# Modulation products on four column tiles of the array, their shifts and scales kept as columns, in a two-layer diffusion step

## The reference

```
mod = silu(cond) @ w_mod[l] + b_mod[l]            # 2 layers x (1024 x 6144), 50 MB of weights
sh1, sc1, g1, sh2, sc2, g2 = split(mod, 6)
hn = rmsnorm(x, norm1_g[l]) * (1 + sc1) + sh1
x = x + g1 * mixer(hn)                            # layer 0: RG-LRU and short conv; layer 1: attention
hn = rmsnorm(x, norm2_g[l]) * (1 + sc2) + sh2
x = x + g2 * channel_mixer(hn)                    # layer 0: SwiGLU; layer 1: top-2 of 8 experts
```

## Time and profile before

| | us |
|---|---|
| timed runs | 1918.38, 1922.94, 1922.93 (median 1922.93) |
| profiled execution | 1918.46, span 1916.8 |
| TensorE, VectorE, ScalarE, GpSimd busy | 1765.3, 1119.7, 914.7, 104.1 |
| mean granted TensorE clock | 0.959 of full speed |

### The profile page before, as it was taken

One profiled execution on the slowest core, in us unless ns is written; L12 is line 12 of the kernel. 1 busy time (PEld: TensorE's weight loads), 2 busy tenths in 40 slices (PEclk: granted clock), 3 DMA queues, 4 the chain that ended last, 5 costly groups with the idle time before them and its releaser, 6 DMA issues.

```text
span 1916.8 us, 22046 instructions
## 1 busy us (share of the span) xinstructions
PE 1765.3 (92%) x8208; PEld 1344.4 (70%) x8208; DVE 1119.7 (58%) x1022; ACT 914.7 (48%) x943; POOL 104.1 (5%) x86
## 2 busy tenths in 40 slices
PE   6999989699999969999978999999999999999992
PEld 2444444378888869877366878787878787878781
DVE  0310650443332354245167797979797979797976
ACT  1203210333332242222026686868686868686864
POOL 2211010000000011000000000000000000000001
PEclk9999999899999979998958999999999999999996
DMA  9766547923332372240057899999999999999994
GB/s 298 242 220 220 177 140 257 332 74 132 109 104 62 143 147 95 70 151 1 21 198 258 305 394 351 395 351 395 351 395 350 395 351 395 351 393 352 395 350 149
DMA packets 278410, 472.94 MB, mean 247 GB/s; under 512 B 32876, under 2 KB 133896, under 8 KB 278360
## 3 DMA queue, kind: packets, MB, share of 16 engines
q1 hardware_dynamic: 254704, 438.33, 64.5%
q10 hardware_dynamic: 19160, 20.51, 3.2%
q0 software_dynamic: 4496, 13.41, 1.9%
HBM read 454.28 MB, written 17.93 MB: 246 GB/s over the span
## 4 chain that ended last, share of the span: by engine, by line
PE 80%; DVE 9%; ACT 4%; issue 3%; ACTq 2%; DMA 1%; DVEq 0%; POOL 0%; POOLq 0%
PE ps L1803 26%; PE ps L1816 10%; PE ps L1602 10%; PE ps L1526 8%; PE ps L1567 5%; PE ps L1619 5%; PE ps L1499 4%; PE ps L1658 3%; DVE e_lo L1361 2%; PE ps L1581 2%; ACTq L869 2%; ACT e_hi L994 2%; PE ps L1673 2%; PE ps L1725 1%; PE ps L1697 1%
## 5 line engine op out<-in xcount | busy, mean ns | idle before, releaser
L1361 DVE TENSOR_TENSOR e_lo<-e_raw,e_hi 128x2048 fp32r<-128x2048 f32 (+1 forms) x330 | 690.7, 2115 | 117.6 <-ACT e_hi L994 114.3
L994 ACT ACTIVATE e_hi<-e_raw 128x2048 fp32r<-128x2048 f32 (+1 forms) x330 | 580.6, 1774 | 127.3 <-PE ps L1803 90.4
L1803 PE MATMUL ps<-e_hi,e_x 128*128 128x512 f32 (+1 forms) x1728 | 511.7, 376 | 7.1 <-DVE e_x L1456 7.1
L1803 PEld LDWEIGHTS ps<-e_hi,e_x 128*128 128x128 f32 x1728 | 316.8, 189 | 66.7 <-issue 10.8
L1803 PE MATMUL ps<-e_lo,e_x 128*128 128x512 f32 (+1 forms) x864 | 322.1, 373 | 0.0
L1816 PE MATMUL ps<-e_hi,e_h 128*128 128x512 f32 x792 | 221.8, 391 | 0.0
L1803 PEld LDWEIGHTS ps<-e_lo,e_x 128*128 128x128 f32 x864 | 163.6, 189 | 27.0
L1602 PE MATMUL ps<-split,hi_x 128*128 128x512 f32 (+1 forms) x576 | 171.8, 383 | 5.4 <-DVE lo_x L1247 5.4
L1816 PEld LDWEIGHTS ps<-e_hi,e_h 128*128 128x128 f32 x792 | 147.6, 188 | 29.6
L1526 PE MATMUL ps<-ring,cond 128*2 128x256 f32 x576 | 128.6, 384 | 8.7 <-DMA ring<-in_w_mod_dram 8.7
L1816 PE MATMUL ps<-e_lo,e_h 128*128 128x512 f32 x396 | 122.2, 390 | 0.0
(11 more groups left out here) (236 smaller groups left out, 1896.0 us busy)
## 6 DMA issues: line engine op xcount, KB each, us to landing
e_raw<-in_moe_w_gate_dram SPq DMA_DIRECT2D x94, 1024.0 KB, 11.0
e_raw<-in_moe_w_up_dram SPq DMA_DIRECT2D x92, 1024.0 KB, 11.2
e_raw<-in_moe_w_down_dram SPq DMA_DIRECT2D x90, 1024.0 KB, 11.2
ring<-in_w_mod_dram SPq DMA_DIRECT2D x36, 1024.0 KB, 6.1
mod_extra<-in_w_mod_dram SPq DMA_DIRECT2D x12, 1024.0 KB, 6.4
ring<-in_w_qkv_dram SPq DMA_DIRECT2D x6, 2048.0 KB, 8.9
ring<-in_w_in_dram SPq DMA_DIRECT2D x5, 2048.0 KB, 10.1
ring<-in_ffn_w_gate_dram SPq DMA_DIRECT2D x10, 1024.0 KB, 7.6
```

Of the source, the lines that this page charges most:

```text
L994: act.activation(high_part(c), raw(c), ACT.Copy).then_inc(hi_ok, 1)
L1361: dve.tensor_tensor(low_part(c), raw(c), high_part(c).bitcast(F32), ALU.subtract).then_inc(lo_ok, 1)
L1803: ins = pe.matmul(out, e_x[:, xt, ci, :], wt[:, kk, :], start=(ci == 0 and m == 0), stop=(ci == KC - 1 and m == 2))
```

## The change

The modulation product is laid out anew.

- A unit is 1 MB of 512 columns and half the contraction (four chunks of 128), so the moving rows in DRAM are 2 KB long rather than 1 KB. `cond` is padded with zeros to 32 columns per chunk.
- A block `b` of 512 columns is two units. Chunk k of a unit writes PSUM partitions 32k to 32k+31, which puts it on column tile k of the array. A unit has four products of 512 columns, and each tile adds its two chunks.
- The four partial rows lie in partitions 0, 32, 64, 96 (and the next ones, for the second group). ScalarE copies the whole 128 x 512 bank to `mod_part`. TensorE then sums the partials with a 0/1 matrix (`mod_sums`): for gates as a 2 x 512 row; for shifts and scales with `mod_part` as weights, so that columns come out at once. ScalarE takes these sums to `mod_row` or `modv`.
- GpSimd adds biases to four gate rows and stores those alone; biases of shifts and scales are added as columns.
- Two groups' worth (four blocks) precede the x projection, and four blocks now follow each of x, c, v, b and g. The raw tokens are transposed into `hn_t` early and scaled in place when the columns are there.
- PSUM bank 5 belongs to the sums, and PB becomes 5.

```diff
-GROUP = 4 * 256
+MOD_BLOCKS = 2 * MODS // 512
+LAST_TAKE = 11
-        MOD_SPLIT = {"x": (4, 6), "c": (6, 8), "v": (8, 10), "b": (10, 12), "g": ()}
+        MOD_SPLIT = {"x": (4, 8), "c": (8, 12), "v": (12, 16), "b": (16, 20), "g": (20, 24)}
+        def is_row(b):
+            return b // 2 % 3 == 2
-        PB = 6
+        PB = 5
...
+            def mod_block(b):                                  # SP
+                for n in (2 * b, 2 * b + 1):
+                    if n >= 4:
+                        sp.wait_ge(mod_used, n - 3)
+                    wl, at_ = w_mod[b // 12].rearrange(kview, p=P), b % 12 * 512
+                    sp.dma_start(mod_unit(n), wl[:, n % 2 * 4:n % 2 * 4 + 4, at_:at_ + 512]).then_inc(mod_full[n % 4], 16)
...
+            for r in range(4):                                 # GpSimd
+                at_ = (3 * r + 2) * GROUP
+                pool.dma_start(mod_bias, bias_rows[at_:at_ + GROUP].partition_broadcast(2)).then_inc(mod_bias_in, 16)
+                pool.wait_ge(mod_bias_in, 16 * (r + 1))
+                pool.wait_ge(mod_taken, 3 * r + 2)
                 pool.tensor_tensor(mod_row, mod_row, mod_bias, ALU.add).then_inc(mod_row_ok, 1)
...
+            def take_sums(b):                                  # ScalarE
+                if not is_row(b) and (b % 6 != 3 or b < 6):
+                    return
+                act.wait_ge(mod_sum, b + 1)
+                if is_row(b):
+                    if b >= 6:
+                        act.wait_ge(mod_stored, 16 * (b // 6))
+                    ins = act.activation(mod_row[:, b % 2 * 512:b % 2 * 512 + 512], ps[0:2, 5, :], ACT.Copy)
+                else:
+                    c_ = 8 * (b // 2 - 1)
+                    ins = act.activation(modv[:, c_:c_ + 16, :].rearrange("p m g -> p (m g)"), ps[:, 5, 0:32], ACT.Copy)
+                ins.then_inc(mod_taken, 1)
+            def mod_out(*blocks):
+                for b in blocks:
+                    if b >= 2:
+                        if b != 12:
+                            take_sums(b - 2)
+                        act.wait_ge(mod_sum, b - 1)
+                    act.wait_ge(mod_used, 2 * b + 2)
+                    act.activation(mod_part[:, b % 2, :], ps[:, 6 + b % 2, :], ACT.Copy).then_inc(mod_copied, 1)
...
-                    act.wait_ge(mod_stored, 16 * (2 * MODS // GROUP))
+                    act.wait_ge(mod_stored, 16 * 4)            # gate_in(0)
-            mods_before = {"c": (4, 5), "gate": (6, 7), "g": (10, 11)}
+            mods_before = {"c": (4, 5, 6, 7), "gate": (8, 9, 10, 11), "g": (16, 17, 18, 19)}
-                        mod_out(8 + d)
+                        mod_out(12 + 2 * d, 13 + 2 * d)
+            mod_out(20, 21, 22, 23)
+            take_sums(22)
+            take_sums(23)
             gate_in(0)
...
+            def mod_block(b):                                  # TensorE
+                if b >= 2:
+                    pe.wait_ge(mod_copied, b - 1)
+                for n in (2 * b, 2 * b + 1):
+                    pe.wait_ge(mod_full[n % 4], n // 4 * 16 + 16)
+                    for k in range(4):
+                        ins = pe.matmul(ps[32 * k:32 * k + 32, 6 + b % 2, :], cond[:, n % 2 * 4 + k, :],
+                                        mod_unit(n)[:, k, :], start=(n % 2 == 0), stop=(n % 2 == 1))
+                    ins.then_inc(mod_used, 1)
+            def mod_sums(b):
+                pe.wait_ge(mod_copied, b + 1)
...
+                if is_row(b):
+                    ins = pe.matmul(ps[0:2, 5, :], sum_up, mod_part[:, b % 2, :], start=True, stop=True)
+                else:
+                    for n in range(4):
+                        o = 2 * (4 * (b % 6) + n)
+                        ins = pe.matmul(ps[:, 5, o:o + 2], mod_part[:, b % 2, n * P:(n + 1) * P], sum_up,
+                                        start=True, stop=True)
+                ins.then_inc(mod_sum, 1)
+            def mod_blocks(lo, hi):
+                for b in range(lo, hi):
+                    mod_block(b)
+                    if b > lo:
+                        mod_sums(b - 1)
```

More of the change, by code:

```diff
@@ L85 @@
 C_EXP2, C_ROW2 = C_ROW + 8, C_ROW + 24
-N_CONST = C_ROW2 + 16
+C_SUM = C_ROW2 + 16
+N_CONST = C_SUM + 2
 WORK = 18560
@@ L128, in shape_constants @@
         k[:, C_ROW2:][:, at_] = np.arange(8) * (P * TILES) + P * t
+    for g in range(2):
+        k[g::32, C_SUM + g] = 1.0
     return k
@@ L308, in hybrid_step @@
         mod_ok = sem("mod_ok")
-        mod_copied, mod_bias_in, mod_row_ok, mod_stored, mod_in = (sem("mod_" + n) for n in
-            ("copied", "bias_in", "row_ok", "stored", "rows_in"))
+        mod_copied, mod_sum, mod_taken, mod_bias_in, mod_row_ok, mod_stored = (sem("mod_" + n) for n in
+            ("copied", "sum", "taken", "bias_in", "row_ok", "stored"))
+        raw_dve, raw_act, cond_zero = sem("raw_turn_dve"), sem("raw_turn_act"), sem("cond_zeroed")
         gains_ok = sem("gains_ok")
@@ L521, in fill @@
                 sp.dma_start(dst, src).then_inc(ring_full[slot_of(n)], 16)
[L523 to L535, removed]
+            def mod_block(b):
[4 more added lines that the diff above has]
+                    sp.dma_start(mod_unit(n), wl[:, n % 2 * 4:n % 2 * 4 + 4, at_:at_ + 512]).then_inc(mod_full[n % 4], 16)
+            sp.wait_ge(s_vec, 16 * 13)
+            for b in range(4):
+                mod_block(b)
             win = w_in[0].rearrange(kview, p=P)
@@ L539, in _ @@
                 fill(F_IN + f, slab(F_IN + f), win[:, :, g * 512:(g + 1) * 512])
[L540 to L545, removed]
+                for b in range(*MOD_SPLIT["xcvbg"[f]]):
+                    mod_block(b)
             for f in range(2):
@@ L735, in _ @@
                 rows.append((vec_rows[COL[name]:COL[name] + src.shape[0], 0, :], src))
+            rows.append((vec_rows[0:2 * MODS // P, 1, :], b_mod.rearrange("l (r p) -> (l r) p", p=P)))
             for dst, src in rows:
@@ L895, in _ @@
             act.wait_ge(st_t, 1)
+            act.wait_ge(mod_ok, 2)
             split_high_ffn(0)
@@ L1530, in turn_mod_rows @@
-            def turn_mod_rows(n_rows, count, bank):
-                pe.wait_ge(mod_in, count)
-                for g in range(2):
-                    ins = turn(ps[:, bank, g * P:g * P + n_rows], vec_rows[0:n_rows, g, :])
-                ins.then_inc(vec_t, 1)
+            def mod_block(b):
[7 more added lines that the diff above has]
+                    ins.then_inc(mod_used, 1)
```

160 lines of the change are left out of this document (88 added, 72 removed).

## The result

The changed kernel takes **1884.15 us** (median of four runs, 1881.78 to 1887.33) against 1920.66 for the kernel before in the same comparison (1917.34 to 1922.94): a ratio of 0.9816, 95% interval 0.980 to 0.983. The profiled execution took 1887.33 us. The forecast was 1885. The first residual starts at 328.27, 33.3 us earlier than before; from there to the end the profiled span is 1557.3 us against 1555.2, so the whole gain lies ahead of that residual, as argued. But some of the forecast's sizes are off, in opposite directions, and it took the experiments to show that.

What follows compares the result with a forecast made beforehand. TensorE's modulation products were taken to bound the serial start, with DMA bounding the stages after the change. Stage terms summed to -37.0, plus 4 for clock: -33 on 1918.46 us, 1885 us, range 1870 to 1898 (1866 to 1913 with the clock rival).

Steps and rivals of the forecast that it cites:

- start to x projection: Before the first projection: eight units instead of sixteen and no trip through DRAM, x projection at 42.4 instead of 80.74, -38.3 us.
- after x: Stage after the x projection: refilled units and the next slab bound by their loads, 20.45 us against 27.72, -7.3.
- after c to the last gate: Stage after the c projection: gates wait for ScalarE's copy, table load and evacuations, 28.7 us against 38.9, -10.2.
- last gate to the end of b: From v through b: ScalarE's second direction starts earlier, -7.1; a third b item follows v's first evacuation, +5.2; together -1.9 us.
- after b: Stage after the b projection: the same as after x, bound by loads of units and slab, -7.3 us.
- after g to the gate loads: After g: four blocks, sums, GpSimd's add and the row store now precede ScalarE's gate loads, 28.0 us against 0, +28.0.
- zeroing: ScalarE's nine zeroing DMAs behind the gate loads, ahead of the first FFN split: length left at 37.19 us, no change.
- projections x, c, g: Clock lost after new waits ahead of a projection or product (after x, b, g): 2.7 us at half of three, +4.
- unit's size: TensorE's time for one unit of four products: pairs of records overlap only partly, 1.7 us instead of 3.46.
- side estimate of 1.45 us: TensorE's time for one unit if 3.46 us is divided by the Trainium skill's 2.38 for three column tiles.
- rival with four at once: All four products of a unit overlap, 0.86 us a unit: about -6.7, 1879 us; inside the forecast's 0.62 chance.
- clock rival: TensorE's clock falls in the waits, so refilled units run at half clock: +18, 4 already counted, 1899 us; chance 0.16.

Runs made afterwards that it cites:

- spare products: The changed kernel with unread identity products, two ahead of each refilled unit and four ahead of the slab after x and b: 1878.67 us, ratio 0.979.

## Why the prediction was right, step by step

Measured from the profiles of before and after, in us against the kernel before:

| step | predicted | measured |
|---|---|---|
| start to x projection (80.74 to 43.48) | -38.3 | -37.3 |
| after x (27.7 to 20.8) | -7.3 | -6.9 |
| after c to the last gate (38.9 to 30.4) | -10.2 | -8.6 |
| last gate to the end of b (78.5 to 72.5) | -1.9 | -6.0 |
| after b (27.7 to 21.2) | -7.3 | -6.5 |
| after g to the gate loads (0 to 28.0) | +28.0 | +28.0 |
| zeroing (37.2 to 33.2) | 0 | -4.0 |
| projections x, c, g (predicted: the clock behind three waits) | +4 | +8.1 |
| **first residual** | **-33** | **-33.3** |

The rows measured leave 0.1 over, which lie between the gate loads and the residual.

**The mechanism held.** TensorE's products left the path, DMA took it, the row path after g ran over the store, GpSimd and the zeroing, and the product (279.82, 20.3 after g, predicted 20.45) stayed ahead of the split. (It was to wait for its slab; that landed at 279.5, and the profile puts the last 0.5 us down to ScalarE's take of a gate row.) The prediction named 42 for the x projection, 322 for the split and 329 for the residual: 43.48, 322.55 and 328.27.

**The unit's size was wrong.** The step "those two must follow each other, and products are issued in order, so the second record of one can run beside the first of the next and no more" gave 1.7 us, which is what two tiles measure (1.75). Four tiles measure 0.87. TensorE's weight loads at the start of the stage, in the kernel after:

```profile
67.15 0.13 PEld L1560 LDWEIGHTS ps<-ring,work 128*32 128x32 f32 x4 [0.30 <-issue]
67.58 0.13 PEld L1560 LDWEIGHTS ps<-ring,work 128*32 128x32 f32 x4 [0.30 <-issue]
68.01 0.13 PEld L1560 LDWEIGHTS ps<-ring,work 128*32 128x32 f32 x4 [0.30 <-issue]
```

Four weight loads go every 0.43 us, which is one record of 512 columns (3.44 / 8 on one tile): four records run side by side, and the pair of a product does not hold up its neighbours. The Trainium skill, TensorE: Matmul & The Clock Gate, Part 3 (Packing small matmuls), gives 2.38 times for three column tiles, from which the prediction's side estimate of 1.45 us came; here two give 3.44 / 1.75 = 2.0 and four 3.46 / 0.87 = 4.0, and the runs decide; none has three.

**Why that hardly showed: luck.** The rival with four at once took 6.7 us off the forecast for the smaller unit, and on two tiles, where a unit does need what the forecast assumed, the kernel is about 7 us slower (1891.17 against 1884.15). So the forecast's other terms with the right unit would have given 1879, and the kernel with the forecast's unit would have met 1891: the other terms together were some 6 us too low, and that the sum met the time is chance.

Two of them were too low, in part for the clock. The stages after x, c, b and g took 8 us more (1.2, 3.4, 1.6 and 1.7) than the forecast's terms give for them with the right unit. Some of the refilled units run at half clock (two of four after x, three of four after c), with rows of 1.93 us where on two tiles they take 1.91 at full clock (1.00 from 75.36 to 85.20 there), so that such a unit gains nothing by the third and fourth tile. With the spare products the four stages are 3 us shorter together; the other 5 no run takes apart. And the x, c and g projections cost 8.1 where 4 were charged: x is 2.3 longer, behind a wait that the sum did not charge, the first sixteen records of c (7.84 us) and g (7.03) take 2.6 and 1.8 more than 5.25, a quarter of 21.01, and 1.5 are sums that now stand inside c and g. The two smaller terms below pull the other way, together by some 7. The clock rival (1899) had the mechanism but priced it too high: it took every refilled unit to be slow, and 2.7 us each at c, g, v and the product, where v (20.9 us for 64 records) and the product (41.44 for 96) ran at full clock.

**Two smaller terms.** From the last gate to the end of b the -1.9 was -7.1 and +5.2; measured are -7.9, -1.7 and +3.6. ScalarE's second direction begins its work 28.1 after the last gate, against 36.0 before. Not the copies of v's blocks release it, as the sum had it (they end at 166.73, 24.5 after the last gate, and the table load behind them at 168.02), but VectorE's scans of the first direction, which took 5.91 us where they took 3.95 before:

```profile
164.37 5.91 DVE L1237 TENSOR_TENSOR_SCAN work<-work 128x386 f32<-128x386 f32 x4
```

From there to v's first evacuation it is 1.7 us shorter (170.37 to 197.24, against 225.36 to 253.94), as the scans of the second direction are. The third item behind the evacuation did come, but the three took 15.7 us at full clock, since b's first item, run early, had the slow records (7.22 us); before, two items behind the wait took 13.31. And the zeroing, left at its length, needed 4.0 less; no run settles why. In the runs that keep it on ScalarE's list it takes 27.1 to 33.3 us.

What stays open: the rest of the program, from the residual on, is 2.1 us longer in this one profile, which is within what the runs differ by among themselves (1881.78 to 1887.33).

## What to carry to other kernels

A product with few output columns took as long here as its moving columns did (3.46 us for eight of 256, 3.44 for four of 512 on one tile); spread over four column tiles it became four times as cheap, and the question turned at once into which load, in which place of its queue, ends the stage. When an engine's work leaves the path, look at what was hidden behind it: here a slab at the end of SP's list (7 to 9 us, by the gains over the kernel before or by the medians), zeroing DMAs in ScalarE's list (7 to 10) and blocks behind the last projection that fit into a gap (10 to 13), 22 to 25 us in one kernel where the change itself gave 36. And charge the clock of an engine that is emptied: with the waits filled, the first residual came 5.5 us earlier, not much less than the 7 that the third and fourth tile gave. A total that meets the time does not prove its terms: here errors of 4 to 7 us cancelled.

## What the hardware showed that was not expected

- Four float32 products of 512 columns, each two records, on four column tiles: 0.87 us, against 1.75 on two and 3.44 on one.
- TensorE with more work was sooner done: spare products in the waits raised the granted clock of the stage after x from 0.79 to 1.00, and brought 5.5 us at the first residual; where no wait is, they cost time (6.6 us before b).
- Of the eight scans of 386 columns, four for each direction, some take 0.97 us and some 2.9: before, the first direction's four took 3.95 and after 5.91, with the second's shorter by 1.7. No run here was made to explain it.
